# One decoder layer with a routed mixture of experts: odd blocks gathered as quarter rows and turned by VectorE, even blocks turned by TensorE, and the scatter issued ahead of the gather

## The chip, the cores and the metric

The kernel runs on one core of one Trainium2 chip. The metric is the device time of one execution in microseconds (us), the median of several runs. The core has TensorE (matrix products), VectorE, ScalarE and GpSimd (elementwise work; GpSimd also issues indirect DMAs) and SyncE, whose queue (SP) issues the plain DMAs; 16 DMA engines carry all transfers.

## The reference

It is a decoder layer over 2048 tokens of 1024 features: sliding-window attention beside a gated recurrence, an output projection, a LayerNorm, and then a mixture of experts (MoE). All but the MoE is computed in stages that the change touches only by one more store. The part that matters:

```
h = LayerNorm(alpha * x + mixer(x))
scores, 8 experts of 64 for each token, weights w[token, expert]
routed[token] = sum over its 8 experts e of w * (silu(h @ w_gate[e]) * (h @ w_up[e])) @ w_down[e]
out = LayerNorm(alpha * h + shared_expert(h) + routed)
```

D_EXPERT is 256, so w_gate[e] and w_up[e] are 1024 x 256 and w_down[e] is 256 x 1024, in float32.

## The kernel before

**Stages.** `mixer` (to about 500 us), `output_and_route` (output projection, LayerNorm, scores and routing; it stores each tile of h and its 64 pair weights as rows of a DRAM table `htab`, 1024 + 64 numbers per token), `place_and_share` (it computes where each token-expert pair goes, and the shared expert of eight tiles), `experts` (from about 853 to 2385 us) and `share_and_norm`.

**Blocks.** The 16384 pairs are sorted by expert and cut into blocks of 128 pairs, each of one expert; an expert has as many blocks as it needs, 162 in this run. `idx` holds for each block and partition the row of `htab`; a `table` holds a word per block with its expert, the next expert, the rank and whether it is the first block of its expert. The loop `turns` does two blocks per turn: step k = 0 is an even block, k = 1 an odd one. With b the block of a step:
- GpSimd copies the indices of block b+4 into `gi[k]` (L2298), issues the gather of its 128 rows into `xg[k]` (L2301, `x_in[k]`), copies the scatter's indices into `si[k]` (L2319), waits for both halves of y of block b and for `added` of the other parity (the scatter of block b-1 has landed), and issues the scatter with addition into `acc` (L2326, `added[k]`). Two scatters may not be in flight, as both can hold one token.
- TensorE, step b: low part of the gate/up product of b+1 (`gate_up_low`, L2514), down product of b (L2559, twelve products of 512 columns into the two halves of psY), high part of gate/up of b+2 (`gate_up_high`, L2503), the turn of H of b+1 (L2521) and the turn of x of b+3 (`turn_x`, L2487: eight transposes of 128 x 128 into psX).
- ScalarE: HT_hi (L2389), xT_hi of b+2 from psX (L2340, two of 512), silu of b+1 (L2376), the high halves of the next expert's weights where a first block comes (L2344), and the first half of y (L2395).
- VectorE: HT_lo (L2466), xT_lo of b+2 (L2406), `pair_weight` (L2434), `product` for H of b+1 (L2443), then `split` (L2409, the low part of the weights, 2048 elements each): the first of three where b+2 is the first block of an expert, then the second half of y (L2476), then the second, and the third for the block before.

All products are made of a high and a low part (float32r), three products for one. The weights lie in raw_gu and raw_d (two slots, loaded on SP's queue as soon as a slot's splits are done), the split ones in gu_split, d_hi, d_lo (two slots). xg, y, psG and H have two buffers, psY, psX (two halves) and sg one. Each engine works through its own list in order; semaphores tie the lists together.

## Time and profile before

| | us |
|---|---|
| median of 3 runs | 2494.95 (2492.94 to 2497.22) |
| the profiled execution | 2485.66 |
| its span, first to last instruction | 2483.8 |
| TensorE busy | 2382.5 (96%) |
| VectorE busy | 1575.5 (63%) |
| ScalarE busy | 1161.9 (47%) |
| GpSimd busy | 767.3 (31%) |
| mean granted clock of TensorE | 0.985 |

Busy time of TensorE is that of pipelined products with modelled ends: one of 512 columns shows 0.39 us, while the next starts 0.23 us after it. So a stretch is measured from start to start. GpSimd's busy time for an indirect DMA is that of the instruction, not of the transfer.

### The profile page before, as it was taken

The page shows a single profiled execution, that of the slowest core. Times are in us where ns is not written, and L with a number is a line of the kernel's source. Part 1 is how long each engine was busy: PE and PEld are TensorE (multiplying, and loading weights), DVE is VectorE, ACT ScalarE, POOL GpSimd, SP SyncE. Part 2 cuts the span into 40 slices and gives each one's busy share as a digit, 9 for nine tenths or more (in the row PEclk, how much of TensorE's full clock was granted, in tenths as well). Part 3 has the DMA queues.
Part 4 walks back from the last instruction along what each step waited for, and adds up shares of the span by engine and source line. Part 5 has one row for each costly group of instructions (what it writes and reads, how often), then busy time and mean ns, then how long its engine had stood idle before and what let it go on. Part 6 is the DMA issues. An engine that isn't in the chain of part 4 may idle for free. (4 is left out here: it accounts for less than half of the span.)

```text
span 2483.8 us, 49979 instructions
## 1 busy us (share of the span) xinstructions
PE 2382.5 (96%) x11840; PEld 1954.7 (79%) x11842; DVE 1575.5 (63%) x2285; ACT 1161.9 (47%) x1621; POOL 767.3 (31%) x829
## 2 busy tenths in 40 slices
PE   8899999989997799999999999999999999999986
PEld 6677777678886688888888888888888888888875
DVE  6686867768878756555665555656665556655447
ACT  4525253542225645445554445545554445544334
POOL 0010100011110134334543433534443334444327
PEclk9999999989998899999999999999999999999998
DMA  7242323364445579778988878888888789987863
GB/s 254 77 144 98 111 94 111 117 218 164 171 164 206 196 230 284 223 219 270 273 259 233 254 218 263 268 266 262 257 253 243 224 223 274 283 247 222 216 221 136
DMA packets 253808, 524.34 MB, mean 211 GB/s; under 512 B 18065, under 2 KB 165169, under 8 KB 249649
## 3 DMA queue, kind: packets, MB, share of 16 engines
q1 hardware_dynamic: 204464, 336.64, 39.7%
q0 software_dynamic: 48672, 186.86, 29.4%
q8 instruction: 36, 0.59, 0.1%
q14 instruction: 28, 0.22, 0.0%
q10 hardware_dynamic: 608, 0.02, 0.0%
HBM read 386.61 MB, written 136.87 MB: 211 GB/s over the span
## 5 line engine op out<-in xcount | busy, mean ns | idle before, releaser
L2503 PE MATMUL psG<-gu_split,xT_hi 128*128 x2624 | 624.3, 390 | 2.9 <-ACT xT_hi L2340 1.5
L2503 PEld LDWEIGHTS psG<-gu_split,xT_hi 128*128 128x128 f32 x2624 | 493.8, 188 | 106.2 <-issue 3.6
L2326 POOL DMA_INDIRECT acc<-y,si x162 | 290.1, 1791 | 728.6 <-DMA acc<-y,si 413.3
L2409 DVE TENSOR_TENSOR gu_split<-raw_gu,gu_split (+1 forms) x127 | 290.6, 2288 | 175.3 <-ACT gu_split L2344 171.7
L2514 PE MATMUL psG<-gu_split,xT_lo 128*128 x1304 | 339.3, 402 | 5.9 <-issue 5.8
L2514 PEld LDWEIGHTS psG<-gu_split,xT_lo 128*128 128x128 f32 x1304 | 233.1, 188 | 50.1 <-issue 8.7
L2344 ACT ACTIVATE gu_split<-raw_gu x126 | 234.3, 1907 | 33.5 <-issue 33.5
L2301 POOL DMA_INDIRECT xg<-htab,gi x164 | 205.0, 1250 | 130.4 <-POOL gi L2298 109.7
L2409 DVE TENSOR_TENSOR d_lo<-raw_d,d_hi (+1 forms) x64 | 146.7, 2292 | 149.5 <-ACT d_hi L2344 149.5
L2389 ACT ACTIVATE HT_hi<-psH 128x256 fp32r<-128x256 f32 x162 | 62.4, 385 | 351.6 <-PE psH L2521 351.6
L2406 DVE TENSOR_TENSOR xT_lo<-psX,xT_hi 128x512 fp32r<-128x512 f32 x328 | 209.7, 680 | 8.5 <-ACT xT_hi L2340 8.5
L2476 DVE COPY y<-psY 128x512 f32<-128x512 f32 x162 | 111.4, 688 | 154.0 <-PE psY L2559 154.0
L2559 PE MATMUL psY<-d_hi,HT_hi 128*128 x648 | 199.9, 390 | 0.0
L2559 PE MATMUL psY<-d_lo,HT_hi 128*128 x648 | 199.7, 389 | 0.0
L2559 PE MATMUL psY<-d_hi,HT_lo 128*128 x648 | 199.6, 389 | 0.0
L2340 ACT ACTIVATE xT_hi<-psX 128x512 fp32r<-128x512 f32 x328 | 178.5, 596 | 17.6 <-PE psX L2487 9.2
L2487 PE MATMUL psX<-ident,xg 128*128 128x128 f32 x1320 | 171.7, 273 | 4.2 <-PEq L1639 4.2
L2376 ACT ACTIVATE sg<-psG 128x256 f32<-128x256 f32 x163 | 62.6, 384 | 204.3 <-PE psG L2514 204.3
L2344 ACT ACTIVATE d_hi<-raw_d (+1 forms) x64 | 122.7, 1917 | 74.6 <-PE psY L2559 74.5
L2487 PEld LDWEIGHTS psX<-ident,xg 128*128 128x128 f32 x1320 | 149.3, 141 | 4.7 <-issue 4.6
L2466 DVE TENSOR_TENSOR HT_lo<-psH,HT_hi 128x256 fp32r<-128x256 f32 x162 | 67.8, 418 | 131.0 <-ACT HT_hi L2389 130.5
L2395 ACT ACTIVATE y<-psY 128x512 f32<-128x512 f32 x162 | 95.6, 590 | 102.5 <-PE psY L2559 98.4
(388 smaller groups left out, 3723.7 us busy)
## 6 DMA issues: line engine op xcount, KB each, us to landing
raw_gu<-in_w_gate_dram SPq DMA_DIRECT2D x64, 1024.0 KB, 6.0
raw_gu<-in_w_up_dram SPq DMA_DIRECT2D x64, 1024.0 KB
raw_d<-in_w_down_dram SPq DMA_DIRECT2D x64, 1024.0 KB, 6.9
wring<-split_d SPq DMA_DIRECT2D x24, 1024.0 KB, 4.8
split_d<-wring POOLq DMA_DIRECT2D x8, 1024.0 KB, 4.2
raw_d<-mixed SPq DMA_DIRECT2D x16, 512.0 KB, 3.9
xt<-in_x_dram SPq DMA_DIRECT2D x16, 512.0 KB, 4.3
htab<-h SPq DMA_DIRECT2D x16, 512.0 KB, 2.6
```

Source lines behind the costliest of these rows:

```text
L2301: nc.gpsimd.indirect_dma_start(out=xg[slot][:], out_offset=None, in_=htab, in_offset=bass.IndirectOffsetOnAxis(ap=gi[slot][:, 0:1], axis=0 ...
L2326: nc.gpsimd.indirect_dma_start(out=acc, out_offset=bass.IndirectOffsetOnAxis(ap=si[k][:, 0:1], axis=0), in_=y[k][:], in_offset=None, compu ...
L2340: nc.scalar.activation(xT_hi[slot][:, h * HALF:(h + 1) * HALF, :], psX[h][:], ACT.Copy).then_inc(xhi_s[h], 1)
L2344: nc.scalar.activation(dst, src, ACT.Copy).then_inc(done, 1)
L2395: nc.scalar.activation(y[k][:, 0:512], psY[:, 0, :], ACT.Copy).then_inc(y_s[0], 1)
L2406: nc.vector.tensor_tensor(xT_lo[slot][:, at, :], psX[h][:], xT_hi[slot][:, at, :], ALU.subtract).then_inc(xlo_s[h], 1)
L2409: nc.vector.tensor_tensor(dst, src, hi, ALU.subtract).then_inc(dlo_s if n == 2 else gulo_s, 1)
L2476: nc.vector.tensor_copy(y[k][:, 512:], psY[:, 1, :]).then_inc(y_s[1], 1)
L2487: m = nc.tensor.transpose(psX[half][:, c, :], xg[slot][:, (half * HALF + c) * P:(half * HALF + c + 1) * P], ident[:])
L2503: nc.tensor.matmul(psG[slot][:], xT_hi[slot][:, c, :], right[:, bass.ds(w, 1), c, :].rearrange("p a n -> p (a n)"), start=(n == 0 and c == ...
L2514: m = nc.tensor.matmul(psG[slot][:], xT_lo[slot][:, c, :], gu_hi[:, bass.ds(w, 1), c, :].rearrange("p a n -> p (a n)"), start=False, stop= ...
L2559: m = nc.tensor.matmul(psY[:, h, :], left[:, c, :], right[:, bass.ds(w, 1), c, h * 512:(h + 1) * 512].rearrange("p a n -> p (a n)"), start ...
```

## The change

- A second table `hcut` in DRAM holds each token's row again, as four pieces of 256 features and 16 pair weights (272 numbers). `store_h` and the store of the weights write it beside `htab`; its padding rows are zeroed in `place_and_share`.
- `pidx` holds, for each odd block, four indices of pieces per partition: 16 small VectorE instructions in `indices` make it.
- An odd block is gathered by four indirect DMAs of 128 pieces each (`gather_pieces`) into `xg[1]` of another layout. VectorE turns it by 32 x 32 blocks into a new tile xF (`turn_x` of VectorE: one instruction of 1024 elements and one of 128 for the weights), which ScalarE and VectorE then split into high and low from SBUF, in one instruction each. TensorE only turns the weights (`turn_weights`, one transpose into psW), from which `pair_weight` takes its column.
- As VectorE's turn leaves the features in the order 8p + c (partition p, chunk c), the weights of gate and up are loaded in that order ("(p k)"), and TensorE's transposes of even blocks read their columns with a step of eight.
- On VectorE `turn_x` stands in the even step after `product`, ahead of the first split and of y's second half. TensorE turns both the weights and the even block in the odd step.
- GpSimd issues the scatter of block b first and the gather of block b+4 behind it. ScalarE makes the copies of indices (`gather_index`, `scatter_index`).

```diff
+def gather_pieces(nc, hcut, to, at, done):
+    for g in range(QUADS):
+        nc.gpsimd.indirect_dma_start(out=to[:, g, 0:PIECE], out_offset=None, in_=hcut.rearrange("r a w -> (r a) w"),
+                                     in_offset=bass.IndirectOffsetOnAxis(ap=at[:, g:g + 1], axis=0)).then_inc(done, 16)
...
             def store_h(n):
                 sp.dma_start(htab[n * P:(n + 1) * P, 0:D], h[n % 2][:]).then_inc(row_out[n % 2], 16)
+                sp.dma_start(hcut[n * P:(n + 1) * P, :, 0:FEATS], h[n % 2][:].rearrange("p (a w) -> p a w", a=QUADS)).then_inc(row_out[n % 2], 16)
...
+                dve.wait_ge(idx_s, 2)
+                odd = idx[:].rearrange("p (b k) -> p b k", k=2)[:, :, 1]
+                for a in range(QUADS):
+                    for g in range(QUADS):
+                        last = nc.vector.tensor_scalar(pidx[a * QP:(a + 1) * QP, :, g], odd[g * QP:(g + 1) * QP], float(QUADS), float(a),
+                                                       ALU.mult, ALU.add)
...
-                        sp.dma_start(dst, w[0, bass.ds(e, 1)].rearrange("a (k p) n -> p (a k) n", p=P)).then_inc(sm, 16)
+                        rows = "a (k p) n -> p (a k) n" if sm is down_in else "a (p k) n -> p (a k) n"
+                        sp.dma_start(dst, w[0, bass.ds(e, 1)].rearrange(rows, p=P)).then_inc(sm, 16)
...
 GpSimd, body
-                    pool.wait_ge(turned[1], s.n + 3)
-                    pool.wait_ge(pairw_s, s.n + 3)
-                    carry_wait(pool, passed)
-                    gather(s.n + AHEAD, k, s.n + AHEAD + 1)
-                    nc.gpsimd.tensor_copy(si[k][:], idx[:, bass.ds(s.n, 1)]).then_inc(si_s, 1)
                     s.wait(pool, si_s)
                     for h in range(2):
                         s.wait(pool, y_s[h])
                     pool.wait_ge(added[1 - k], (s.turn + k) * 16)
                     nc.gpsimd.indirect_dma_start(out=acc, ...).then_inc(added[k], 16)
+                    pool.wait_ge(next_gi_s, s.n + 1)
+                    if k == 0:
+                        pool.wait_ge(pairw_s[0], s.turn + 2)
+                    if k:
+                        gather_pieces(nc, hcut, xg[1], gi[1], x_in[1])
+                    else:
+                        gather_rows(nc, htab, xg[0], gi[0], x_in[0])
...
 ScalarE
+            def high_x(nth, slot):
+                if slot:
+                    act.wait_ge(odd_turned, nth)
+                    nc.scalar.activation(xT_hi[1][:], xF[:, 0:KC, :], ACT.Copy).then_inc(odd_xhi, 1)
+                    return
...
-                    evac_x(s.n + 3, k)
+                    high_x(s.turn + 2, k)
+                    gather_index(s, k)
...
-                    act.wait_ge(added[k], s.turn * 16)
+                    scatter_index(s, k)
...
 VectorE
+            def turn_x(nth):
+                dve.wait_ge(x_in[1], nth * 16 * QUADS)
+                if not (isinstance(nth, int) and nth == 1):
+                    dve.wait_ge(odd_wturn, nth - 1)
+                    dve.wait_ge(odd_xhi, nth - 1)
+                nc.vector.transpose(xF[:, 0:KC, :].rearrange("p c (g j) -> p c g j", g=QUADS),
+                                    xg[1][:, :, 0:FEATS].rearrange("p g (i c) -> p c g i", c=KC))
+                nc.vector.transpose(xF[:, KC, :].rearrange("p (g j) -> p g j", g=QUADS),
+                                    xg[1][:, :, FEATS:WIDE]).then_inc(odd_turned, 1)
+            def low_x(nth, slot):
+                if slot:
+                    dve.wait_ge(odd_xhi, nth)
+                    nc.vector.tensor_tensor(xT_lo[1][:], xF[:, 0:KC, :], xT_hi[1][:], ALU.subtract).then_inc(odd_xlo, 1)
+                    return
...
-                    for h in range(2):
-                        evac_x(h, s.n + 3, k)
+                    low_x(s.turn + 2, k)
                     s.wait(dve, H_s)
-                    pair_weight(nexts[n + 1], k, s.turn + 2)
-                    product(s.n + 2, 1 - k)
+                    if k == 0:
+                        pair_weight(nexts[n + 1], s.turn + 2, 0)
+                        pair_weight(nexts[n], s.turn + 1, 1)
+                    product(s.n + 2, 1 - k, s.turn + 1 + k)
+                    if k == 0:
+                        turn_x(s.turn + 2)
                     when_first(dve, nexts[n + 1], lambda: split(nexts[n + 1], 0))
                     s.wait(dve, yps_s[1])
                     dve.wait_ge(added[k], s.turn * 16)
...
 TensorE
-                    pe.wait_ge(x_in[1 - k], (s.turn + k + 2) * 16 )
-                    carry_wait(pe, passed)
-                    for h in range(2):
-                        pe.wait_ge(xlo_s[h], s.n + 3)
-                        turn_x(1 - k, h)
+                    if k:
+                        turn_weights(s.turn + 2)
+                        turn_x(s.turn + 3)
```

## Rows read from the trace of the kernel before

**Rows 1.** The page: span, busy time by engine, then clock and DMA in 40 slices.

```profile
span 2483.8 us, 49979 instructions
...
PE 2382.5 (96%) x11840; PEld 1954.7 (79%) x11842; DVE 1575.5 (63%) x2285; ACT 1161.9 (47%) x1621; POOL 767.3 (31%) x829
...
PEclk9999999989998899999999999999999999999998
DMA  7242323364445579778988878888888789987863
```

**Rows 2.** Windows: the middle of the expert loop, busy time by engine.

```profile
core 0: us, PE busy (x) PEld busy (x) DVE busy (x) ACT busy (x) POOL busy (x), PEclk, DMA share, GB/s
1100.00:2300.00 1200.00, 1194.96 (x5911) 1002.23 (x5910) 700.58 (x925) 601.70 (x797) 503.92 (x514) 1.00 0.86 251
```

**Rows 3.** Timeline of TensorE over one block: start, length, line, operation.

```profile
1500.39 3.79 PE L2503 MATMUL psG<-gu_split,xT_hi 128*128 x16
1504.03 0.38 PE L2521 MATMUL psH<-ident,H 128*128 128x128 f32 x2
1504.24 1.04 PE L2487 MATMUL psX<-ident,xg 128*128 128x128 f32 x8
1505.04 2.07 PE L2514 MATMUL psG<-gu_split,xT_lo 128*128 x8
1506.95 0.62 PE L2559 MATMUL psY<-d_hi,HT_hi 128*128 x2
...
1509.67 3.79 PE L2503 MATMUL psG<-gu_split,xT_hi 128*128 x16
```

**Rows 4.** The scatter's line: number, first and last start, what ended the waits.

```profile
L2326 POOL DMA_INDIRECT acc<-y,si x162: 1583/1607/2717, 878.4 to 2381.2; - x162
its engine sat idle before it (us, times) until:
  DMA acc<-y,si: 413.3, 77
```

**Rows 5.** Timeline of GpSimd: scatters (L2326) and gathers (L2301).

```profile
1479.25 1.61 POOL L2326 DMA_INDIRECT acc<-y,si  x1 [4.48 <-DVE pairw L2434]
...
1486.87 2.69 POOL L2326 DMA_INDIRECT acc<-y,si  x1 [3.81 <-DVE y L2476]
...
1498.76 1.61 POOL L2326 DMA_INDIRECT acc<-y,si  x1 [6.65 <-DVE pairw L2434]
...
1506.97 1.60 POOL L2326 DMA_INDIRECT acc<-y,si  x1 [4.41 <-DMA acc<-y,si]
...
1509.58 1.01 POOL L2301 DMA_INDIRECT xg<-htab,gi  x1 [0.80 <-POOL gi L2298]
...
1514.70 2.69 POOL L2326 DMA_INDIRECT acc<-y,si  x1 [3.91 <-PE psX L2487]
...
1526.79 1.60 POOL L2326 DMA_INDIRECT acc<-y,si  x1 [6.89 <-DMA acc<-y,si]
```

**Rows 6.** The page, costliest groups: count, busy us, mean ns, idle before.

```profile
L2409 DVE TENSOR_TENSOR gu_split<-raw_gu,gu_split (+1 forms) x127 | 290.6, 2288 | 175.3 <-ACT gu_split L2344 171.7
...
L2406 DVE TENSOR_TENSOR xT_lo<-psX,xT_hi 128x512 fp32r<-128x512 f32 x328 | 209.7, 680 | 8.5 <-ACT xT_hi L2340 8.5
L2476 DVE COPY y<-psY 128x512 f32<-128x512 f32 x162 | 111.4, 688 | 154.0 <-PE psY L2559 154.0
...
L2376 ACT ACTIVATE sg<-psG 128x256 f32<-128x256 f32 x163 | 62.6, 384 | 204.3 <-PE psG L2514 204.3
```

**Rows 7.** The page, DMA issues: the store of h, us to landing.

```profile
htab<-h SPq DMA_DIRECT2D x16, 512.0 KB, 2.6
```

**Rows 8.** Timeline: a small VectorE instruction on the indices.

```profile
840.26 0.22 DVE L1947 TENSOR_SCALAR idx<-zr,blockno 128x4 int32<-128x4 f32 x1
```

**Rows 9.** DMA engines from 1508 to 1520 us, in 40 slices of 0.3 us.

```profile
DMA  0009964789999999989530000000000922778999
```

**Rows 10.** Timeline of VectorE around a y and a split.

```profile
1485.20 0.68 DVE L2476 COPY y<-psY 128x512 f32<-128x512 f32 x1
1485.80 2.28 DVE L2409 TENSOR_TENSOR gu_split<-raw_gu,gu_split  x1
```

**Rows 11.** Windows where the expert loop starts; the columns of rows 2.

```profile
845.00:852.00 7.00, 3.17 (x12) 2.10 (x12) 2.61 (x8) 0.00 (x0) 0.78 (x1) 1.00 0.91 307
852.00:858.00 6.00, 3.70 (x13) 2.95 (x14) 4.39 (x4) 4.04 (x4) 0.00 (x0) 0.59 0.18 37
858.00:864.00 6.00, 6.00 (x27) 4.86 (x26) 3.82 (x4) 2.93 (x3) 2.37 (x2) 0.84 1.05 360
```

More of the change, by code:

```diff
@@ L1271, in store_weights @@
                              wrow[r % 2][:, 0:w, :]).then_inc(wt_out[r % 2], 16)
+                for i in range(w):
+                    sp.dma_start(hcut[(t + i) * P:(t + i + 1) * P, :, FEATS:PIECE],
+                                 wrow[r % 2][:, i, :].rearrange("p (a e) -> p a e", a=QUADS)).then_inc(wt_out[r % 2], 16)
             def load_feature(n):
@@ L2128, in _, with load_expert, experts @@
                     down(n)
[L2131 removed]
+def load_expert(eng, w_gate, w_up, w_down, expert, slot, wgu, wd, loaded, by_run=False):
     for w, sm, dst in zip((w_gate, w_up, w_down), loaded, (wgu[:, slot, :, 0:FE], wgu[:, slot, :, FE:], wd[:, slot])):
[L2134 to L2137 removed]
+        rows = "(p k) n -> p k n" if by_run and w is not w_down else "(k p) n -> p k n"
+        eng.dma_start(dst, w[0, expert].rearrange(rows, p=P)).then_inc(sm, 16)
+def experts(nc, passed, w_gate, w_up, w_down, ident, htab, hcut, acc, table, n_turns, idx, pidx, tails_s, xg, gi, gi_s, x_in, acc_out, gu, guhi_s, gulo_s, wgu, wd, loaded, y, si, added,
             prefetch_shared, prefetch_hT):
@@ L2175, in experts @@
         xlo_s = [sem(f"xlo_s{i}") for i in range(2)]
-        pairw_s = sem("pairw_s")
+        odd_turned = sem("odd_turned")
+        odd_wturn = sem("odd_wturn")
+        odd_xhi = sem("odd_xhi")
+        odd_xlo = sem("odd_xlo")
+        next_gi_s = sem("next_gi_s")
+        pairw_s = [sem(f"pairw_s{i}") for i in range(2)]
         dhi_s = sem("dhi_s")
@@ L2483, in _, with turn_x, turn_weights, gate_up_high @@
         def _(pe):
-            def turn_x(slot, half):
-                for c in range(HALF):
-                    m = nc.tensor.transpose(psX[half][:, c, :], xg[slot][:, (half * HALF + c) * P:(half * HALF + c + 1) * P], ident[:])
-                m.then_inc(turned[half], 1)
-            def gate_up_high(nth, slot, entry):
-                for h in range(2):
-                    pe.wait_ge(xhi_s[h], nth)
+            def turn_x(nth):
+                pe.wait_ge(x_in[0], nth * 16)
+                carry_wait(pe, passed)
+                rows = xg[0][:, 0:D].rearrange("p (q c) -> p c q", c=KC)
+                for h in range(2):
+                    if not (isinstance(nth, int) and nth == 1):
+                        pe.wait_ge(xlo_s[h], nth - 1)
+                    for c in range(HALF):
+                        m = nc.tensor.transpose(psX[h][:, c, :], rows[:, h * HALF + c], ident[:])
+                    m.then_inc(turned[h], 1)
+            def turn_weights(nth):
+                pe.wait_ge(odd_turned, nth)
+                if not (isinstance(nth, int) and nth == 1):
+                    pe.wait_ge(pairw_s[1], nth - 1)
+                carry_wait(pe, passed)
+                nc.tensor.transpose(psW[:], xF[:, KC, :], ident[:]).then_inc(odd_wturn, 1)
+            def gate_up_high(nth, slot, entry, seen):
+                if slot:
+                    pe.wait_ge(odd_xhi, seen)
+                else:
+                    for h in range(2):
+                        pe.wait_ge(xhi_s[h], seen)
                 pe.wait_ge(gulo_s, entry.rank() * 2)
@@ L2505, in gate_up_high, with gate_up_low @@
                                          start=(n == 0 and c == 0), stop=False)
-            def gate_up_low(nth, slot, entry):
-                for h in range(2):
-                    pe.wait_ge(xlo_s[h], nth)
+            def gate_up_low(nth, slot, entry, seen):
+                if slot:
+                    pe.wait_ge(odd_xlo, seen)
+                else:
+                    for h in range(2):
+                        pe.wait_ge(xlo_s[h], seen)
                 w = entry.slot()
```

188 lines of the change are left out of this document (111 added, 77 removed).

## The prediction

> **What bounds the kernel now.** I read the page first, for where the time lies, then the stages, then one period of the expert loop engine by engine, and last who waits for whom on GpSimd. The page shows TensorE busy almost everywhere at full clock [rows 1], and in the 1200 us in the middle of the expert loop it is busy 99.6% of the time, with VectorE at 58%, ScalarE at 50% and the DMA engines at 86% [rows 2]. The reader is to see that nobody but TensorE is full there. One period of the loop (one block of 128 pairs) is 1509.67 - 1500.39 = 9.28 us of TensorE without a hole: 3.64 us for the 16 high gate/up products, 0.21 for turning H, 0.80 (1504.24 to 1505.04) for the eight transposes of x, 1.91 for the low ones, 2.72 for the down ones [rows 3]. A pair of blocks costs TensorE 18.56 us.
>
> There is a second chain that is nearly as long. The 162 scatters start from 878.4 to 2381.2, so one per 9.33 us, 18.67 per pair. GpSimd waits most for the landing of the scatter before (413.3 us in 77 waits), as each scatter waits for `added` of the other parity [rows 4]. From one scatter's start to the next are 7.6, 11.9, 8.2, 7.7 and 12.1 us [rows 5]: a clean one needs about 8.2, and the next can't start sooner. So scatters leave one after the other, far behind their y, but this costs nothing today, because y has two buffers and TensorE never waits for them.
>
> **The change part by part.** TensorE. An odd block loses eight transposes (0.80 us) and gains one for the weights (about 0.10, an eighth of that): -0.70 us per pair, 81 pairs, -57 us if TensorE stays the bound. It would then want 17.86 us per pair.
>
> The even block's transposes now read xg with a step of eight elements. No row shows a strided weight load; the bounds are nothing and one more 0.80 us per pair (the same eight at half speed, taken from the packed ones, [rows 3]). I take nothing, since by the loop below TensorE has room.
>
> VectorE. The odd block's two subtractions from PSUM (2 x 0.68) become one of 1024 elements from SBUF. By the rows of 512 (0.68) and 2048 elements (2.29) an element costs 1.05 ns and an instruction 0.14, so 1.22 us. The two new transposes of 1024 and 128 elements come to 1.22 + 0.28 = 1.5 us [rows 6]. No row shows a VectorE transpose or a strided read; the bounds are 0.7 (the larger at twice the pace) and 2.6 (the larger as long as a 2048 row, at half pace). I take 1.5, the row rate. In sum +1.4 us per pair at 58% busy: no bound by throughput, but what matters is where it stands.
>
> By the Trainium skill ("SBUF — State Buffer", section Door 1: The DMA port swizzle) SBUF is read in lines of 16 bytes, and a stream that moves to a new line with each access pays a penalty. Here each step is 32 bytes, so that rule speaks for the 2.6 and for the slower even transposes, and by it the sum below would be 1.1 us per pair higher; no row of this trace shows it.
>
> ScalarE gets two copies of a few indices per block. Its smallest row here is 0.38 us (sg), so under 0.8 us at 50% busy: hidden, also if they took twice that [rows 2, 6]. One 1024 copy for two of 512 gives some of it back.
>
> GpSimd. The two index copies go. The odd gather becomes four DMAs, each over 128 indices. One gather instruction takes 1.0 us and a scatter 1.6 [rows 5], so the four take 4.0 unless the number of bytes matters (the same 544 KB in all; bounds 1.0 and 4.0). By throughput this is nothing: 1.6 + 1.6 + 1.0 + 4.0 = 8.2 us in 18.7.
>
> DMA: the same bytes in 384 more packets per pair. The second table `hcut` is written in the stage before, from some 500 to 750 us, where the DMA engines are four to six tenths busy [rows 1]: hidden. If that cover were gone, 16 stores of 512 KB at 2.6 us each [rows 7] would cost 42 us. The weights "by run" keep 1 KB pieces at the SBUF side: nothing. The setup gains 16 small VectorE instructions ahead of the odd gather at 0.22 each [rows 8], 3.5 us, and on SP's queue four small DMAs ahead of the weights: +5 us.
>
> **The step that decides: a ring that closes.** At present a gather is issued ahead of the scatter, early in a block, for a block that is turned two steps on; nothing behind it on TensorE comes near it. After the change:
> - GpSimd issues the scatter of odd block O, then the four pieces for O+4.
> - VectorE's turn_x in the very next step, of even block E = O+1, waits for these pieces (it waits for x_in[1] at turn + 2 gathers, and the turn before has issued only that many). Behind this wait in VectorE's queue stand the first split of the next expert, the second half of y of block E, and the other splits.
> - The scatter of E waits for this y, and the scatter of the next odd block, O' = E+1, for the landing of E's.
> So scatter O, pieces, turn_x, y(E), scatter E, scatter O' is a ring, once per pair, with nothing double-buffered in it. Its length from rows:
> 1. Scatter O's start to the data of a gather behind it: the DMA engines carry scatter and gather of 1506.97 and 1509.58 from 1508.9 to 1514.3 (slices of 0.3 us), and are idle then [rows 5, 9]: 7.3 us after the scatter's start. In the new order the first piece can be issued at +1.6, the last at +4.6, where the gather now starts at +2.6. Bounds +0 and +2.0 (the last piece); I take +1.0: 8.3.
> 2. Landing seen by the waiting engine: 1.0, as from y's end at 1485.88 to the scatter's start at 1486.87 [rows 5, 10]; no row shows it for a gather. Bounds 0.5 and 1.5.
> 3. turn_x 1.5 (0.7 to 2.6).
> 4. The first split between it and y: 2.29 in 64 of 162 steps (half of the 127), so 0.9 on the mean [rows 6].
> 5. y's second half 0.69 [rows 6], and 1.0 to the scatter [rows 10].
> 6. Scatter E to scatter O': 8.2 clean. Where splits run just behind y (1485.80) the scatter takes 2.69 instead of 1.60 and the next comes 11.9 later, 3.7 more [rows 5, 10]; in the new order splits still stand right behind y(E). The mean of all is 9.33 and takes in waits for y. I take 8.8; bounds 7.6 and 9.7.
> Sum: 8.3 + 1.0 + 1.5 + 0.9 + 1.7 + 8.8 = 22.2 us per pair, against 18.67 now. That is +3.53 us x 81 = +286 us, with the setup +291.
>
> The Trainium skill ("GPSIMD Engine Reference", section Key points) has GpSimd and VectorE share their way to SBUF, with contention where VectorE has two SBUF inputs. The trace agrees in the scatter of 2.69 us beside a split [rows 5, 10]; the change makes the odd block's subtraction such an instruction too, which could only lengthen the ring.
>
> The ends of the ring: 7.3 + 0.5 + 0.7 + 0.9 + 1.6 + 7.6 = 18.6 (all low), and 9.3 + 1.5 + 2.6 + 0.9 + 1.8 + 9.7 = 25.8 (all high). The terms are independent, so both ends are unlikely; 20.0 to 24.3 holds most of it. TensorE then idles some 4 us per pair. A longer period leaves the DMA engines more room, which pulls down a little.
>
> The profiled execution took 2485.7 us (span 2483.8), 9.3 under the median of the runs: 2485.7 + 291 + 9 = 2786. For the emptier DMA engines I round down to 2780.
>
> **The rivals.**
> - *The ring fits into TensorE's time (the other side).* It decides at a ring of 17.9 us: if the pieces' data came within about 6 us of the scatter and a scatter landed within 7, VectorE would hardly wait. Speaking for it: single steps of 7.6 [rows 5]. Against it: even all low ends give 18.6. Then the time is 2495 - 57 + 5 = 2443. Chance 0.08.
> - *The scatters alone pace it.* turn_x waits little, but the two scatter steps stay at 9.2 to 9.33 each, so TensorE's 0.70 turns into a wait for y buffers: 18.4 to 18.7 per pair, 2478 to 2500. The 413 us of waits speak for it. Chance 0.05.
> - *Strided reads at half pace.* As the likeliest case, but turn_x 2.6: 23.3 per pair, +89, 2870. Chance 0.25. (This is what the 16-byte rule of the Trainium skill, "SBUF — State Buffer", would do in the ring.)
> - *TensorE's clock falls in the new gaps.* Where the loop starts, after stretches with TensorE busy 3.2 of 7 and 3.7 of 6 us, the granted clock reads 0.59 and 0.84 [rows 11], between 1.2 and 2.4 GHz, while it is 1.00 through the gapless loop. TensorE's share of a pair between y(E) and the next y(E) is 2.72 + 3.64 + 1.1 + 1.91 + 2.72 = 12.1 us [rows 3], 24.2 at the lower level, beyond the ring's 22.2. If half of the loop ran so: 23.2 and more, 2880. Chance 0.10.
> - *The ring as summed*, 2690 to 2860. Chance 0.37. *A short ring* of 19 to 21 us (pieces cheap, few splits in the way): 2525 to 2690, chance 0.15.
>
> **How the numbers follow.** Slower in all but the first two rivals: 0.87; a measurement of this kernel tells about 0.2% (5 us) from no change. Of the second rival I give 0.03 to the same and 0.02 to faster; faster 0.10. The range leaves out the first two rivals and the tail of the long rings: 2590 to 2930.
>
> **What would show it.** In the profile after: VectorE's transposes idle for several us ahead of them, ended by the DMA of xg; y's second half late in even steps only; scatters at unequal steps, about 9 us from even to odd and 13 from odd to even; TensorE idle ahead of the down products of odd blocks, for y; its busy share in the loop near 80%; pieces of about 1.0 us each on GpSimd. The prediction is wrong if TensorE stays above 98% busy in the loop, or if the pieces land before VectorE comes to turn_x.

## The result and the profile after

The changed kernel takes 3090.86 us (median of 4 runs, 3085.3 to 3094.66), the kernel before 2493.94 on the same chip (2487.02 to 2497.22): a ratio of 1.2396 with a 95% interval of 1.2363 to 1.2429. It is 597 us slower. The prediction said 2780, with a range up to 2930: the sign and the forecast ring held, the size did not, and a second ring was not foreseen. Of the experiments below one execution, of `scatter_first_alone`, fell into a slower state of the chip (3470.98 us at a granted clock of 0.65) and is left out of its figures.

The page of the changed kernel, for [rows 1]: span, busy time, clock and DMA.

```profile
span 3083.5 us, 49372 instructions
...
PE 2567.3 (83%) x11266; PEld 2026.3 (66%) x11268; DVE 1771.6 (57%) x2382; ACT 1186.8 (38%) x1863; POOL 897.4 (29%) x755
...
PEclk9999999999989888888898988888888888888989
DMA  5323227566466666566666666656565567765654
```

The window of [rows 2], with its columns, after:

```profile
1100.00:2300.00 1200.00, 959.06 (x3886) 756.88 (x3886) 604.24 (x702) 443.19 (x705) 421.53 (x320) 0.88 0.63 180
```

TensorE is busy 80% of a window in which it was busy 99.6%, the granted clock reads 0.88 instead of 1.00, and the DMA engines went from 86% to 63%: nobody is full, so the time is set by a chain. The chain of waits in the loop (1000 to 2900 us; engine, what it waited for, us, times, longest):

```profile
POOL acc L2370 <- DMA acc<-y,si: 372.5, 57, 7.5
POOL acc L2370 <- DVE y L2574: 363.5, 45, 9.9
...
DVE xF L2482 <- DMA xg<-hcut,gi: 252.4, 65, 9.7
...
PE psX L2592 <- DMA xg<-htab,gi: 215.8, 64, 4.8
```

Two waits are new. VectorE waits for the pieces ahead of its transpose, as forecast. TensorE waits for the even block's rows (L2592), nearly as often, and the prediction had no term for that. The predicted ring in the timeline of GpSimd, for [rows 5]:

```profile
1722.12 1.63 POOL L2370 DMA_INDIRECT acc<-y,si  x1 [7.56 <-DVE y L2574]
...
1731.86 2.67 POOL L2370 DMA_INDIRECT acc<-y,si  x1 [5.96 <-DVE y L2574]
1734.83 1.00 POOL L1647 DMA_INDIRECT xg<-hcut,gi  x1 [0.30 <-issue]
1736.14 0.95 POOL L1647 DMA_INDIRECT xg<-hcut,gi  x1 [0.30 <-issue]
1737.39 0.95 POOL L1647 DMA_INDIRECT xg<-hcut,gi  x1 [0.30 <-issue]
1738.64 0.95 POOL L1647 DMA_INDIRECT xg<-hcut,gi  x1 [0.30 <-issue]
1748.79 2.70 POOL L2370 DMA_INDIRECT acc<-y,si  x1 [9.19 <-ACT gi L2404]
...
1759.13 1.59 POOL L2370 DMA_INDIRECT acc<-y,si  x1 [6.36 <-DMA acc<-y,si]
```

and in VectorE's, for [rows 10]:

```profile
1745.03 2.00 DVE L2482 STREAM_TRANSPOSE xF<-xg 128x1024 f32<-128x1024 f32 x1 [9.07 <-DMA xg<-hcut,gi]
1746.94 0.28 DVE L2484 STREAM_TRANSPOSE xF<-xg 128x128 f32<-128x128 f32 x1
1747.13 0.66 DVE L2574 COPY y<-psY 128x512 f32<-128x512 f32 x1
1747.71 2.28 DVE L2498 TENSOR_TENSOR d_lo<-raw_d,d_hi  x1
```

Read it as one chain: odd scatter 1731.86, last piece issued 1738.64, VectorE idle until 1745.03, transpose, y done 1747.79, even scatter 1748.79 (1.00 later), odd scatter 1759.13. The even scatter's wait is put down to ScalarE's gi, but y ended 1.00 ahead of it. Over 78 pairs, worked out from the trace's records of instructions and packets, every even scatter follows its y at 1.0 us (78 of 78), while the odd one mostly follows the landing of the even one and only in 13 cases its own y; a pair takes 26.04 us (+7.37 x 81 = +597, the whole loss).

### The profile page after: what moved, and what is told of

Read it like the earlier page. It is cut to its first block and busy times, and to the rows that moved or that the text cites. A ratio compares the mean times of both kernels' runs of the same rounds, so it can differ in the third digit from the quotient of the medians.

```text
span 3083.5 us, 49372 instructions
## 1 busy us (share of the span) xinstructions
PE 2567.3 (83%) x11266; PEld 2026.3 (66%) x11268; DVE 1771.6 (57%) x2382; ACT 1186.8 (38%) x1863; POOL 897.4 (29%) x755
## 3 DMA queue, kind: packets, MB, share of 16 engines
q0 software_dynamic: 52656, 186.88, 23.6%
## 5 line engine op out<-in xcount | busy, mean ns | idle before, releaser
L2370 POOL DMA_INDIRECT acc<-y,si x162 | 344.3, 2125 | 1237.1 <-DVE y L2574 419.6
L2633 PE MATMUL psG<-gu_split,xT_lo 128*128 x1304 | 431.6, 484 | 70.6 <-issue 70.4
L2633 PEld LDWEIGHTS psG<-gu_split,xT_lo 128*128 128x128 f32 x1304 | 292.5, 236 | 155.1 <-issue 94.8
L1647 POOL DMA_INDIRECT xg<-hcut,gi x332 | 320.7, 966 | 101.1 <-issue 100.6
L2482 DVE STREAM_TRANSPOSE xF<-xg 128x1024 f32<-128x1024 f32 x82 | 176.1, 2148 | 277.3 <-DMA xg<-hcut,gi 277.3
L2592 PE MATMUL psX<-ident,xg 128*128 128x128 f32 x664 | 129.7, 358 | 234.1 <-DMA xg<-htab,gi 230.5
L2498 DVE TENSOR_TENSOR gu_split<-raw_gu,gu_split (+1 forms) x127 | 289.4, 2279 | 49.6 <-ACT gu_split L2416 42.0
L2592 PEld LDWEIGHTS psX<-ident,xg 128*128 128x128 f32 x664 | 106.8, 207 | 249.0 <-issue 249.0
L2495 DVE TENSOR_TENSOR xT_lo<-psX,xT_hi 128x512 fp32r<-128x512 f32 x164 | 110.1, 689 | 244.1 <-ACT xT_hi L2397 244.0
L2671 PEld LDWEIGHTS psY<-d_hi,HT_hi 128*128 128x128 f32 x648 | 135.8, 216 | 130.1 <-issue 100.4
L2397 ACT ACTIVATE xT_hi<-psX 128x512 fp32r<-128x512 f32 x164 | 94.5, 597 | 301.6 <-PE psX L2592 301.4
L2537 DVE SCALAR_TENSOR_TENSOR H<-psG,pairw,sg 128x256 f32<-128x256 f32 x163 | 78.7, 483 | 219.3 <-ACT sg L2448 218.8
L2498 DVE TENSOR_TENSOR d_lo<-raw_d,d_hi (+1 forms) x64 | 146.3, 2286 | 91.1 <-ACT d_hi L2416 91.1
L2671 PEld LDWEIGHTS psY<-d_hi,HT_lo 128*128 128x128 f32 x648 | 127.5, 205 | 81.3 <-issue 56.1
```

The source lines that it names most:

```text
L1647: nc.gpsimd.indirect_dma_start(out=to[:, g, 0:PIECE], out_offset=None, in_=hcut.rearrange("r a w -> (r a) w"), in_offset=bass.IndirectOffs ...
L2370: nc.gpsimd.indirect_dma_start(out=acc, out_offset=bass.IndirectOffsetOnAxis(ap=si[k][:, 0:1], axis=0), in_=y[k][:], in_offset=None, compu ...
L2397: nc.scalar.activation(xT_hi[0][:, h * HALF:(h + 1) * HALF, :], psX[h][:], ACT.Copy).then_inc(xhi_s[h], 1)
L2482: nc.vector.transpose(xF[:, 0:KC, :].rearrange("p c (g j) -> p c g j", g=QUADS), xg[1][:, :, 0:FEATS].rearrange("p g (i c) -> p c g i", c=KC))
L2495: nc.vector.tensor_tensor(xT_lo[0][:, at, :], psX[h][:], xT_hi[0][:, at, :], ALU.subtract).then_inc(xlo_s[h], 1)
L2498: nc.vector.tensor_tensor(dst, src, hi, ALU.subtract).then_inc(dlo_s if n == 2 else gulo_s, 1)
```

## The experiments

Each ran beside the kernel before on its chip (2487 to 2494 us in all calls); times without an interval are single runs. "Ahead" and "behind" mean GpSimd's order of issue. Differences under some 10 us between runs on different chips mean little, as the kernel before itself differs by 7.

**1. The order undone in the changed kernel (`gather_first`).** On GpSimd the block with `wait next_gi_s ... gather_pieces / gather_rows` goes back ahead of `wait si_s, y_s, added ... scatter`.

> Undoes the order on GpSimd alone: the gather for the block four on is issued ahead of the scatter again, all else as in the changed kernel. Ring theory: in the changed kernel scatter O, pieces, turn_x, y(E), scatter E, scatter O' take 10.65 + 2.34 + 0.96 + 0.67 + 1.00 + 10.42 = 26.04 us per pair. With the gather first the pieces go out while the scatter of E still flies, so the ring is open and a pair costs what the two scatters need, 18.4 to 20 us: 2480 to 2600 us. Rival (VectorE's transposes of 2.15 us and the four pieces cost the time wherever they stand): near 3000 us, with VectorE waiting for pieces as before.

Measured: 2588.98, ratio 1.041 (1.0373 to 1.0446). 502 of the 597 us are gone: they hang on the order. 95 stay (102 against the kernel before on this run's own chip).

**2. The order alone, in the kernel before (`scatter_first_alone`).**

```
-  pool.wait_ge(turned[1], s.n + 3) ... gather(s.n + AHEAD, k, s.n + AHEAD + 1)
   ...scatter, .then_inc(added[k], 16)
+  pool.wait_ge(turned[1], s.n + 3) ... gather(s.n + AHEAD, k, s.n + AHEAD + 1)
```

> The kernel before, with GpSimd's order alone changed: scatter first, then the gather (one gather of whole rows, TensorE turns all blocks). Theory, a ring needs pieces for the very next step: here a block is turned two steps after the gather is issued, so the loop from a scatter through its gather to the block's products and scatter runs over more steps and does not close within TensorE's time: 2485 to 2510 us. Rival, the order alone costs the time, whatever VectorE does: 2600 us or more, with TensorE idle for the DMA of xg.

Measured: 3000.78 (three executions), ratio 1.2047 (1.2022 to 1.2072). This fells my theory that only pieces wanted by VectorE in the very next step can close a ring. GpSimd and TensorE in this kernel:

```profile
1699.41 2.68 POOL L2322 DMA_INDIRECT acc<-y,si  x1 [8.55 <-PE psX L2487]
1703.08 1.00 POOL L2301 DMA_INDIRECT xg<-htab,gi  x1 [0.79 <-POOL gi L2298]
1711.11 1.61 POOL L2322 DMA_INDIRECT acc<-y,si  x1 [6.82 <-DMA acc<-y,si]
...
1721.77 1.60 POOL L2322 DMA_INDIRECT acc<-y,si  x1 [6.86 <-DVE y L2476]
```

```profile
1707.30 0.38 PE L2521 MATMUL psH<-ident,H 128*128 128x128 f32 x2
1712.19 1.94 PE L2487 MATMUL psX<-ident,xg 128*128 128x128 f32 x8 [4.51 <-DMA xg<-htab,gi]
1713.78 3.51 PE L2514 MATMUL psG<-gu_split,xT_lo 128*128 x8
1717.13 0.62 PE L2559 MATMUL psY<-d_hi,HT_hi 128*128 x2
```

A second ring: scatter of block n at 1699.41, gather for n+4 at 1703.08, its rows usable at 1712.19 (12.78 after the scatter), eight transposes, and behind them in TensorE's queue the low products and the down products of n+2, y (to 1720.77), scatter of n+2 at 1721.77: 22.36 us for two blocks. Part of it runs at the lower clock: 3.51 us for the low products instead of 2.07 [rows 3], at a granted clock of 0.56 from 1712.0 to 1717.5 us, after TensorE had waited 4.51 us for the rows; what that adds to this ring was not tested by itself. A pair takes 25.1 us on the mean. What was lost is one block of lead: before, the gather 2.6 us behind scatter n is that for n+5 [rows 5], now it is that for n+4. From a gather's issue to TensorE's turn of its rows are 12.5 us on the mean in the kernel before (8.9 at least), and 9.9 here (5.3 at least).

**3 and 4. One ring at a time (`pieces_ahead`, `rows_ahead`).** In the changed kernel only the odd block's pieces, or only the even block's rows, are issued ahead (`if k == 1:` or `if k == 0:` around the gather ahead of the scatter, the other parity left behind it).

> The changed kernel with the odd block's four pieces issued ahead of the odd scatter, as gathers were before; the even block's gather stays behind the even scatter. This opens the predicted ring through VectorE and leaves one through TensorE: even scatter, even gather (its data about 12.4 us after a long scatter's start, 8.6 after a short one's, by the kernel before with the order changed alone), TensorE's turn at the end of the next step, low products, down products, y, the scatter two steps on. Theory V, the predicted ring alone sets the time: 2580 to 2650 us. Theory T, the ring through TensorE is enough: 22.4 to 25 us a pair, 2800 to 3010 us.

> The changed kernel with the even block's gather issued ahead of the even scatter; the odd block's four pieces stay behind the odd scatter. This leaves the ring through VectorE alone. Theory V: 26 us a pair less the even gather's share in the transfers, 2950 to 3090 us. Theory T, TensorE's ring is what holds the changed kernel and VectorE's is shorter: 2600 to 2800 us.

Measured: 2885.52 with TensorE's ring alone, 3026.6 with VectorE's alone. Both rings are real: over the kernel before on their chip they cost 396 and 537 us, and both together 597 (3090.86), so they overlap. Their waits, first pieces ahead:

```profile
PE psX L2602 <- DMA xg<-htab,gi: 197.9, 56, 4.5
```

then rows ahead:

```profile
DVE xF L2492 <- DMA xg<-hcut,gi: 506.3, 65, 9.4
...
PE psY L2681 <- DVE y L2584: 317.3, 67, 6.8
```

Rows ahead is the predicted ring by itself, and there its terms can be read against the forecast: 25.16 us a pair, against 22.2 (below).

**5. More work on TensorE (`longer_tensor`).** `for _ in range(16): nc.tensor.transpose(psW[:], xF[:, KC, :], ident[:])` ahead of the odd block's one.

> The changed kernel with the odd block's transpose of the weights repeated 16 more times: some 1.8 us more work for TensorE in a pair, the result unchanged. Theory, TensorE is off the ring: 3075 to 3105 us. Rival, TensorE's time (or its clock in the gaps) is part of what lengthens the ring: 1.8 x 81 = 145 us more, 3235 us.

Measured: 3085.4, as the theory had it. The granted clock over the whole rises from 0.903 to 0.931 and the time stays. The extra work stands ahead of the wait for the even rows and fills that hole, so TensorE's work there does not set the pace of the changed kernel. Of the clock the run says less: the low products behind the wait follow each other at 0.30 us instead of 0.32 (0.24 before), so that stretch gained little.

**6. One gather for four pieces (`one_gather`).** `gather_pieces` issues one indirect DMA of 1088 elements a row, from htab.

> The changed kernel with the odd block's four gathers of quarter rows replaced by one gather of whole rows (same bytes; the rows then lie packed instead of with gaps, so the transposes' results are not those of the reference). Theory, the three further issues of 1.25 us stand on the ring: from the odd scatter's start to turn_x 10.65 becomes about 8.5 us, 2.1 us a pair or 170 us less, 2920 us. Rival, what turn_x waits for is the transfers behind the scatter's data and not the issues: 3050 us or more.

Measured: 3068.2. My theory failed, the rival held: the 10.65 us between odd scatter and transpose stay 10.5 with one gather, so the issues are not what counts. In rows ahead the fourth piece is issued 5.8 us after the scatter's start, and the scatter's own last packet comes at 7.6; most of the pieces' data follow that (in the changed kernel about two thirds of their packets), to be used at 10.1. The issues are hidden in the scatter's transfers.

**7. Packed reads (`packed_turn`).** `"p g (i c) -> p c g i"` becomes `"p g (c i) -> p c g i"` in the big transpose; the features come out in another order than the even block's.

> The large transpose reads its input packed (step 1 instead of 8 elements); features come out in another order, so the output is not the layer's. If the step of 32 bytes is what makes it 2.15 us, it takes about 1.2 us and the ring is 0.95 us shorter per pair: -77 us, 3010 us. If a transpose of float32 runs at half pace anyway it stays 2.15 and the time 3090. If the transpose is off the ring, the time stays though it gets shorter.

Measured: 3040.6, 50 us less. The group of the transpose, changed kernel and then packed:

```profile
L2482 DVE STREAM_TRANSPOSE xF<-xg 128x1024 f32<-128x1024 f32 x82 | 176.1, 2148 | 277.3 <-DMA xg<-hcut,gi 277.3
```

```profile
L2482 DVE STREAM_TRANSPOSE xF<-xg 128x1024 f32<-128x1024 f32 x82 | 102.0, 1244 | 290.2 <-DMA xg<-hcut,gi 290.2
```

2148 ns with a step of 32 bytes, 1244 packed. By the Trainium skill ("SBUF — State Buffer", section Door 1: The DMA port swizzle) each access that moves to a new 16-byte line pays a penalty. VectorE's two durations agree. 0.9 us off 81 pairs would be 73; 50 came, and the wait ahead of it grew by 13.

**8. turn_x behind y and the splits (`turn_last`).**

```
-                    if k == 0: turn_x(s.turn + 2)        (ahead of the first split)
+                    if k == 0: turn_x(s.turn + 2)        (behind the last split)
```

> VectorE's turn_x moved behind y's second half and the splits, at the end of the even step; GpSimd's order stays (scatter first). Ring theory: y(E) and the scatter of E no longer wait for the pieces. A longer ring is left, scatter O, pieces, turn_x, VectorE's odd step up to y(O), the scatter of O': 10.6 + 2.4 + about 5 + 1.0 = 19 us per pair, so 2500 to 2640 us. Rival (the late pieces themselves cost it, whatever stands behind them): about 3080 us.

Measured: 2883.26, a miss. y(E) no longer waits, but HT_lo of the odd block stands behind turn_x in VectorE's queue, TensorE's down products wait for it (155.2 us in 58 waits), and a pair takes 23.6 us. Which wait closes that ring is not separated. VectorE hardly waits for the pieces any more (68.5 us in 30 waits from 1000 to 2700 us, 227.5 in 58 in the changed kernel), TensorE still waits for the even rows (60.0 us in 33), the odd scatter comes right behind its y in 35 of 78 pairs and the even one in 50, and the time is that of TensorE's ring alone (2885.52). So TensorE's ring may be what is left, with the wait for HT_lo inside it. A wait moved within one queue finds the next customer.

**9. Hardly any weights moving (`small_weights`).** Each load of weights cut to its first chunk (`dst[:, 0:1, :]`: one of eight for gate and up, one of two for down); the products use stale weights.

> Each load of an expert's weights brings one chunk of eight (gate, up) or of two (down) alone; the rest of the buffers keeps old numbers, so the output is not the layer's. In the changed kernel most scatters of even blocks have their first packet 6.3 us after their start instead of 2.2. Theory A (weight loads started by the splits behind y hold the scatter's packets up): first packets at 2.2 us, ring 26.0 - 3.4 - 1.5 to 2.5 = 20 to 21 us, 2600 to 2700 us. Theory B (VectorE's two-input split locks GpSimd out while it makes the descriptors): first packets stay at 6.3, about 3050 us.

Measured: 2954.2, between the two; 137 of the 597 us come back. The trace of the changed kernel separates the two causes. A scatter's first packet comes 2.2 us after its start when nothing disturbs it (30 of 156 scatters), 2.95 where its instruction takes 2.7 us instead of 1.6 and no weights move (6), 5.0 with weights moving beside a short instruction (48), and 6.3 with both (72). "Moving" means here that a packet of the weights' queue is under way 1.5 to 3.5 us after the scatter's start. The long instruction alone puts the first packet off by 0.8 us; the weights have the larger part.

**10 to 14. What the 95 us are that stay with both rings open.** All with the gather ahead, each with one thing more: packed transpose; weights' rows in the old order (`a (k p) n` for `a (p k) n`; features and weights then pair wrongly); turn_x right behind y; one gather of whole rows for four pieces (the transposes then give other features); the three layout changes together (one gather, packed, old order).

> The changed kernel with the gather issued ahead of the scatter, and the big VectorE transpose reading packed elements (the features come out in another order than the even block's). Theory, in this order the scatters' chain of about 19.9 us a pair sets the pace, and turn_x lies beside it: within 20 us of the 2589 of the same kernel with strided reads. Rival, turn_x is still on the path that ends last: 0.9 us a pair less, 2515 us.

> The changed kernel with the gather ahead of the scatter, and the gate and up weights loaded in the order of the kernel before (the products then pair features and weights wrongly). In the kernel with gather first a scatter with weights moving has its first packet 5.1 us after its start, in the kernel before 3.7 to 4.1. Theory, loading the weights by run costs that: about 1.1 us on 75 of 162 scatters, 80 us at most, of which scatters beside a long instruction have no part: 2530 to 2560 us. Rival, the order of the weights' rows in memory is indifferent: within 10 us of 2589.

> The changed kernel with the gather ahead of the scatter, and turn_x moved from ahead of the second half of y to right behind it, ahead of the splits. Theory, the wait of VectorE for the pieces (209 us in 54 waits) then no longer delays y, and the transposes keep the splits off the scatter's start: 2480 to 2560 us, with the scatters' chain setting the pace. Rival, turn_x behind y delays HT_lo and the splits as it did in the last place (2883): 2620 us or more.

> The changed kernel with the gather ahead of the scatter and the odd block's four pieces replaced by one gather of whole rows. Theory, three more issues of 1.25 us and the extra packets lie ahead of the odd scatter and its y: 2530 to 2570 us. Rival, pieces cost nothing where they are issued early: within 8 us of 2589.

> The same with the packed transpose and the weights in the old order as well: all that is left of the change is the turning of odd blocks by VectorE. Theory, the parts add up: 20 + 16 less than the kernel with one gather. If this reaches 2450, VectorE's turning itself is worth its 57 us; if it stays above 2494, turning by VectorE costs time in whatever form it is fed.

| with gather first | us | ratio, 95% |
|---|---|---|
| strided, four pieces | 2588.98 | 1.041 (1.0373 to 1.0446) |
| packed transpose | 2568.87 | 1.0301 (1.0268 to 1.0333) |
| old order of weights | 2572.89 | 1.0345 (1.0322 to 1.0368) |
| turn_x behind y | 2594.85 | 1.0422 (1.0397 to 1.0448) |
| one gather | 2466.11 | 0.9899 (0.9882 to 0.9917) |
| one gather, packed, old order | 2453.78 | 0.9861 (0.9838 to 0.9884) |

It is the pieces: one gather takes 123 us off, far more than I expected, and lands below the kernel before. Of the other forecasts, the packed one held just (20 us), the old order of weights fell between its two (16 us), and turn_x behind y was a miss: it bought nothing. The parts did not add up (36 expected for packed and old order, 12 measured); what sets the pace there is no longer what it was. With all three gone, the turning by VectorE gives 35 us (2488.91 to 2453.78) of the 57 that TensorE saves. The pieces' cost in their place, timeline of GpSimd with gather first:

```profile
1508.84 0.99 POOL L1647 DMA_INDIRECT xg<-hcut,gi  x1 [0.30 <-issue]
1510.14 0.95 POOL L1647 DMA_INDIRECT xg<-hcut,gi  x1 [0.30 <-issue]
1511.39 0.95 POOL L1647 DMA_INDIRECT xg<-hcut,gi  x1 [0.30 <-issue]
1512.64 3.05 POOL L1647 DMA_INDIRECT xg<-hcut,gi  x1 [0.30 <-issue]
...
1529.61 1.85 POOL L1647 DMA_INDIRECT xg<-hcut,gi  x1 [0.30 <-issue]
1531.76 2.49 POOL L1647 DMA_INDIRECT xg<-hcut,gi  x1 [0.30 <-issue]
1534.56 0.94 POOL L1647 DMA_INDIRECT xg<-hcut,gi  x1 [0.31 <-issue]
1535.81 1.63 POOL L2378 DMA_INDIRECT acc<-y,si  x1 [0.30 <-issue]
```

Single pieces take up to 3 us, and the scatter of 1535.81 starts 0.30 behind the last one: it queued behind them, as 23 of 78 odd scatters did. The three long pieces shown each begin while one of VectorE's splits runs:

```profile
1512.59 2.29 DVE L2498 TENSOR_TENSOR d_lo<-raw_d,d_hi  x1 [2.44 <-ACT d_hi L2416]
...
1528.30 2.33 DVE L2498 TENSOR_TENSOR gu_split<-raw_gu,gu_split  x1 [1.61 <-ACT gu_split L2416]
...
1531.15 2.28 DVE L2498 TENSOR_TENSOR gu_split<-raw_gu,gu_split  x1
```

It is so for all of them: of the last 324 pieces in this trace 64 take over 1.15 us, and all 64 begin while a VectorE instruction with two SBUF inputs runs (L2498 or L2490); of the 247 that begin beside none, none is long. Four more issues a pair are four more chances for this meeting. With one gather, VectorE's wait for xg falls from 208.8 us to 52.0.

**15. Hardly any weights, gather first (`gather_first_small_weights`).**

> The changed kernel with the gather ahead of the scatter, each weight load cut to its first chunk (the products use stale weights). Theory, the scatters' chain (19.9 us a pair) sets the pace there, and the weights' transfers lengthen it (first packet 5.1 instead of 2.2 us after the scatter's start in 75 of 156): below 2500 us, down to the 2443 at which TensorE's work would set it. Rival, VectorE's waits ahead of y set the pace: above 2550.

Measured: 2439.03. Its window 1000 to 2300 us (columns of [rows 2]), and that of gather first:

```profile
1000.00:2300.00 1300.00, 1298.49 (x6144) 1071.29 (x6143) 937.92 (x1110) 685.07 (x1110) 702.75 (x507) 1.00 0.69 158
```

```profile
1000.00:2300.00 1300.00, 1217.05 (x5508) 983.24 (x5507) 845.96 (x998) 619.67 (x1000) 639.69 (x454) 0.96 0.83 233
```

TensorE is full again, and the time is near what the prediction's first rival gives (2443). In gather first no engine is full, and two things each give back more than the 95 us: one gather for four (123 us) and smaller transfers of weights (150). So the pieces and the transfers around the scatters set the pace together; the runs do not share it out between them.

**16 to 18. The same four pieces issued earlier.** ScalarE writes their indices in the even step (`gather_index(s, 1)` ahead of the wait for yps_s[0]), and `gather_pieces(..., first, last)` issues pieces first to last:

```
+ if k == 0:  gather_rows(...); gather_pieces(..., 0, m)       ahead of the even scatter
+ else:       gather_pieces(..., m, QUADS)                     ahead of the odd one
```

with m = 4, 2, 1.

> The changed kernel with gathers ahead of scatters, and the odd block's four pieces issued a scatter earlier still: ahead of the even scatter, right behind the even block's rows, as soon as turn_x has freed the buffer. Theory, what costs is where the pieces stand: VectorE's wait for them (209 us) goes, and the odd scatter no longer queues behind them: 2460 to 2530 us, unless the even scatter now queues behind 5 us of pieces. Rival, their number costs: 2570 us or more.

> The same, with two pieces ahead of the even scatter and two ahead of the odd one, so that neither gap between scatters holds more than 4 us of issues. Theory of the place: 2470 to 2540 us, better than all four in one gap if GpSimd's time between scatters matters more than VectorE's wait. Rival, the number: 2570 us or more.

> As pieces in two halves, but one piece ahead of the even scatter and three ahead of the odd one. In two halves the even scatter came behind the landing in only 35 of 78 cases, in the rest right behind a piece's issue; the odd one behind the landing in 74 of 78. Theory, the even gap is overfull and the odd one has room: the step from odd to even scatter falls from 9.36 towards the 8.3 that its landing allows, the time to 2460 to 2495 us. Rival, the third piece in the odd gap lengthens that one and the last pieces come late for turn_x: 2510 to 2590 us.

Measured: m = 4: 2606.48, 1.049 (1.0438 to 1.0541). m = 2: 2505.75, 1.0066 (1.0041 to 1.009). m = 1: 2587.1, 1.0379 (1.0352 to 1.0407). With two and two, 83 of the 95 us are gone, so it is mostly the place of the pieces; their number keeps the other 40 of the 123 us (2505.75 against 2466.11 with one gather). With four in the even gap the even scatter queues behind them (its landing was what it waited for in 2 of 78 cases). The last forecast, 2460 to 2495 us for one and three, missed by 92 us. GpSimd's groups, 1000 to 2300 us, two and two:

```profile
L1647 POOL DMA_INDIRECT xg<-hcut,gi x276 | 385.0, 1395 | 186.0 <-ACT gi L2406 119.9 <-issue 65.6 <-DMA acc<-y,si 0.3
L2380 POOL DMA_INDIRECT acc<-y,si x138 | 252.5, 1830 | 380.2 <-DMA acc<-y,si 350.7 <-issue 29.5
```

and one and three:

```profile
L1647 POOL DMA_INDIRECT xg<-hcut,gi x260 | 356.4, 1371 | 264.9 <-ACT y L2473 104.5 <-ACT gi L2406 93.0 <-issue 62.0
L2380 POOL DMA_INDIRECT acc<-y,si x130 | 248.9, 1915 | 316.6 <-DMA acc<-y,si 262.7 <-issue 40.5 <-DVE y L2579 13.4
```

Long even scatters are 21 of 78 with two and two, 34 with one and three, 44 with gather first; whether that is cause or consequence of the pieces' place stays open. Long pieces are not the measure: two and two has 112 of 324, more than any other of these, and is the fastest. What a long piece costs depends on whether a scatter stands behind it.

## Why the prediction was wrong in its size

**What held.** TensorE's busy share, the wait ahead of VectorE's transposes, y late in even steps, unequal scatter steps, pieces of about 1.0 us, and the sign. The saving on TensorE was as forecast, 0.70 us a pair: measured on TensorE from one block's first high product to that of two blocks on, a pair takes 18.68 us before and 17.97 with gather first and hardly any weights, where the time is 2439.03 against a rival's 2443. The kernel before was not run with small weights; as its TensorE is 99.6% busy in the loop, little could have come of it. Hidden at no cost, as said: ScalarE's copies. The even block's strided transposes too: eight took 1.06 us at 1730.78 in the changed kernel, 1.04 before [rows 3]. Of the DMA only the count was off: the trace has 48 more packets a pair, of 4 bytes each, and not 384; no sum used it.

**The steps that failed** are two, and their shares can be read from the runs: of the 311 us between 2780 and 3090.86, the predicted ring alone has 247 (rows ahead, 3026.6), by three terms of its sum that were too small, and the ring that was not foreseen has the other 64. Each of the two would have carried the time past the forecast by itself (3026.6 and 2885.52 against 2780).

**The ring that was not foreseen** hangs on the sentence that a gather is issued "for a block that is turned two steps on; nothing behind it on TensorE comes near it". By the program it is the next step: step b issues the gather of b+4, and TensorE turns b+4 at the end of step b+1, ahead of the down products that the scatter after next waits for. With the scatter first, 12.78 us lie between a scatter and the turn of the rows behind it in the timeline above, 11.1 on the mean in the changed kernel. I asked for the ring only at the queue that the change rewrote, VectorE's, and not at the one that it left alone. The order alone costs 508 us without any VectorE turn, and the ring through TensorE 297 over gather first in the changed kernel (2885.52 less 2588.98).

**The predicted ring's own terms were too small.** It ran by itself in rows ahead. Means over 78 pairs, worked out from that trace:

| term | predicted | rows ahead | changed kernel |
|---|---|---|---|
| 1 + 2, odd scatter to turn_x | 9.3 | 10.14 | 10.65 |
| 3, turn_x | 1.5 | 2.21 | 2.34 |
| 4, to y(E) | 0.9 | 0.91 | 0.96 |
| 5, y and to the scatter | 1.7 | 1.69 | 1.67 |
| 6, even to odd scatter | 8.8 | 10.21 | 10.42 |
| sum | 22.2 | 25.16 | 26.04 |

25.16 - 18.67 = 6.49 us, x 81 = 526, and 2485.7 + 526 + 5 = 3017 for a profiled execution; rows ahead took 3026.6. So the way from the ring to the time holds within 10 us, and three terms were mis-sized by 0.8, 0.7 and 1.4; the changed kernel's 0.88 more comes with the even rows behind the even scatter, and so with TensorE's ring.

- Term 3: 2.21, between the row rate that I took and the 2.6 that was a rival with 0.25; packed it was 1.24, just the row rate. The strided rival's mechanism was right, and I gave it the lesser chance.
- Term 6: the even scatter is long in 76 of 78 pairs there. In the changed kernel 73 of its 78 long scatters have one of VectorE's splits (L2498, two SBUF inputs) running across their start and the other five the odd subtraction (L2490, two as well); in the kernel before all 26 long ones have (L2409), out of 156. A split stands right behind y(E), and y(E) releases the even scatter 1.0 us later, so the ring makes a chance meeting a fixed one. I had the row of 2.69 us and its 11.9-us step in hand [rows 5, 10], and took the mean over free-running scatters (8.8). The weights' transfers that then run beside the scatter's bear the larger part: the first packet comes at 2.2 us undisturbed, 2.95 by the long instruction alone, 6.3 with both. The weights on the move also add to term 1. The Trainium skill ("GPSIMD Engine Reference", section Key points) has GpSimd and VectorE contend where VectorE has two SBUF inputs. The trace agrees: where such an instruction runs across its start, a scatter of 1.6 us becomes one of 2.7.
- Term 1: not the issues (one gather: -22 us), but the odd scatter's own data: its last packet comes 8.1 us after its start in the changed kernel, ahead of most of the pieces' data.

**The range** failed by calling the terms independent. In the ring three of them erred the same way, and the even scatter's step (10.21) lay beyond its own upper bound of 9.7; the sum of all high ends, 25.8, is near the 25.16 measured. The upper end of 2930 was also lower than the prediction's own 24.3 us a pair, which by its sum gives 2956; 3090.86 lies beyond either. The low end of turn_x, 0.7, left out the smaller transpose of 0.28, which changed nothing here.

**The rivals.** The scatters pacing alone come nearest in gather first, where the even scatter stands right behind a landing in 55 of 78 pairs: there the 95 us were. TensorE's clock did fall, to 0.88; more work in its gaps raised it over the whole and moved nothing, though not much where the low products wait. The short ring and the ring inside TensorE's time did not occur.

**What was not seen at all:** the pieces cost 123 us where they do not close a ring. The prediction called them "nothing" by throughput on GpSimd, and had no term for a scatter that queues behind them or for their meeting with VectorE's splits.

## What to carry to other kernels

When an order of issue is swapped, count the lead that every consumer of the delayed transfer loses, the untouched engines first, and follow each queue round to the scatter again: any loop longer than the period is a new period. In a closed ring do not use mean durations; ask which instruction will always meet which, and take the conflicting case. Several small indirect DMAs cost by where they stand between the serial ones: two and two here gave back 83 of 95 us, four in either gap, or three and one, none or hardly any. And keep them off the moments at which VectorE reads two SBUF operands: here each long piece met one.

## What the runs showed of the hardware

- VectorE's 128x1024 fp32 transpose takes 1.24 us packed and 2.15 with reads 32 bytes apart. TensorE's eight strided weight loads of 128x128 f32 keep the pace (1.06 against 1.04 us): a single load reads 191 ns instead of 140 in the records (gather first with hardly any weights, kernel before), but that stays hidden behind the products.
- Pieces of 128 indices issue every 1.25 us (0.95 and 0.30 between), but single ones take up to 3 us. All of the 64 long ones with gather first begin while a VectorE instruction with two SBUF inputs runs: a mean of 1275 to 1395 ns in the kernels with gathers first, 962 in the changed kernel, where VectorE waits for the pieces meanwhile and none of 324 is long.
- A scatter's first and last packets come later when weights move on the other queue, and a little later when its instruction is long. In the changed kernel, 156 scatters, us after the scatter's start:

| instruction | weights | scatters | first packet | last packet |
|---|---|---|---|---|
| 1.6 us | still | 30 | 2.2 | 5.9 |
| 2.7 us | still | 6 | 2.95 | 6.7 |
| 1.6 us | moving | 48 | 5.0 | 8.4 |
| 2.7 us | moving | 72 | 6.3 | 9.7 |

In the kernel before, the undisturbed ones are the same (2.2), and short ones with weights moving have their first packet at 4.1 on the mean.
